# Decoder layer on one core: four last slabs by token tile, layer norm rows scaled on ScalarE, idle transposes on TensorE, and a first load of x of 256 columns

## What is computed

```python
h = layer_norm(ALPHA * x + 0.5 * swiglu(x, ffn1...), ln1_g, ln1_b)     # "up1", "down1"
mix = hybrid_mixer(h, ...)                                             # "kvdt", "attn", "attn_o", "ssd", "merge", "out"
h = layer_norm(ALPHA * h + mix, ln2_g, ln2_b)
h = layer_norm(ALPHA * h + 0.5 * swiglu(h, ffn2...), ln3_g, ln3_b)     # "up2", "down2"

def layer_norm(x, g, b):
    xc = x - mean(x)
    return xc * rsqrt(mean(xc * xc) + LN_EPS) * g + b
```

## Time and profile before

| | |
|---|---|
| time before, 3 runs | median 2670.36 us (2670.35 to 2671.6) |
| the profiled execution | 2668.99 us, span 2667.4 us |
| PE, PEld busy | 2634.5 us (99%), 2188.8 us (82%) |
| DVE busy | 2002.6 us (75%) |
| ACT busy | 1361.7 us (51%) |
| POOL busy | 130.0 us (5%) |
| chain that ended last | PE 95%, DVE 3%, ACT 1% |
| mean granted clock | 0.996 |

### The profile page before, as it was taken

One profiled execution on the slowest core, in us unless ns is written; L12 is line 12 of the kernel. 1 busy time (PEld: TensorE's weight loads), 2 busy tenths in 40 slices (PEclk: granted clock), 3 DMA queues, 4 the chain that ended last, 5 costly groups with the idle time before them and its releaser, 6 DMA issues.

```text
span 2667.4 us, 36687 instructions
## 1 busy us (share of the span) xinstructions
PE 2634.5 (99%) x12546; PEld 2188.8 (82%) x12546; DVE 2002.6 (75%) x2410; ACT 1361.7 (51%) x1678; POOL 130.0 (5%) x170
## 2 busy tenths in 40 slices
PE   8999999999999999999999999999999999999997
PEld 7888888888787788888888888888878888888886
DVE  6999997688666665677777765444689999977986
ACT  5555555455344454566555554444355555554553
POOL 1000000000000000211111100000000000000000
PEclk9999999999999999999999999999999999999999
DMA  6666566666655546665555565667666665666664
GB/s 224 204 191 209 185 205 204 214 200 204 189 171 147 156 150 197 206 181 179 177 177 177 179 183 165 190 190 247 200 190 204 190 211 186 205 202 229 210 208 171
DMA packets 286195, 513.96 MB, mean 193 GB/s; under 512 B 19648, under 2 KB 52592, under 8 KB 284048
## 3 DMA queue, kind: packets, MB, share of 16 engines
q1 hardware_dynamic: 279552, 485.03, 57.8%
q0 software_dynamic: 4880, 25.36, 2.6%
q10 hardware_dynamic: 1664, 2.26, 0.2%
HBM read 506.23 MB, written 6.36 MB: 192 GB/s over the span
## 4 chain that ended last, share of the span: by engine, by line
PE 95%; DVE 3%; ACT 1%; issue 0%; DMA 0%; POOL 0%; POOLq 0%; SPq 0%; ACTq 0%; DVEq 0%
PE acc L787 13%; PE acc L789 13%; PE acc L788 13%; PE acc L853 5%; PE acc L855 5%; PE acc L854 5%; PE acc L871 4%; PE acc L872 4%; PE acc L873 4%; PE spare L871 4%; PE spare L872 4%; PE spare L873 4%; PE spare L855 3%; PE spare L854 3%; PE spare L853 3%; PE spare L756 2%
## 5 line engine op out<-in xcount | busy, mean ns | idle before, releaser
L1728 DVE TENSOR_TENSOR w_lo<-land,w_hi 128x1024 fp32r<-128x1024 f32 (+1 forms) x956 | 1149.2, 1219 | 499.4 <-ACT w_hi L1309 490.6
L1309 ACT ACTIVATE w_hi<-land 128x1024 fp32r<-128x1024 f32 (+1 forms) x956 | 976.8, 1029 | 916.9 <-PE acc L789 328.0
L787 PE MATMUL acc<-w_hi,a_hi 128*128 128x512 f32 (+1 forms) x1184 | 451.2, 381 | 2.6 <-DVE a_lo L1775 1.8
L789 PE MATMUL acc<-w_hi,a_lo 128*128 128x512 f32 (+1 forms) x1184 | 435.8, 368 | 0.0
L788 PE MATMUL acc<-w_lo,a_hi 128*128 128x512 f32 (+1 forms) x1184 | 434.4, 367 | 0.0
L787 PEld LDWEIGHTS acc<-w_hi,a_hi 128*128 128x128 f32 x1184 | 223.9, 189 | 46.8 <-issue 9.2
L789 PEld LDWEIGHTS acc<-w_hi,a_lo 128*128 128x128 f32 x1184 | 223.6, 189 | 38.2
L788 PEld LDWEIGHTS acc<-w_lo,a_hi 128*128 128x128 f32 x1184 | 224.1, 189 | 37.4 <-issue 3.6
L853 PE MATMUL acc<-w_hi,a_hi 128*128 128x512 f32 x576 | 227.7, 395 | 2.0 <-DVE a_lo L1775 1.7
L855 PE MATMUL acc<-w_hi,a_lo 128*128 128x512 f32 x576 | 225.1, 391 | 0.0
L854 PE MATMUL acc<-w_lo,a_hi 128*128 128x512 f32 x576 | 225.0, 391 | 0.0
(11 more groups left out here) (388 smaller groups left out, 4233.1 us busy)
## 6 DMA issues: line engine op xcount, KB each, us to landing
land<-w_in SPq DMA_DIRECT2D x232, 512.0 KB, 3.9
land<-ffn_w_gate SPq DMA_DIRECT2D x176, 512.0 KB, 3.9
land<-ffn_w_up SPq DMA_DIRECT2D x176, 512.0 KB, 4.3
land<-ffn_w_down SPq DMA_DIRECT2D x176, 512.0 KB, 4.7
land<-w_ssd_o SPq DMA_DIRECT2D x64, 512.0 KB, 4.3
land<-w_in SPq DMA_DIRECT2D x132, 128.0 KB, 2.3
land<-w_attn_o SPq DMA_DIRECT2D x32, 512.0 KB, 4.1
land<-w_out SPq DMA_DIRECT2D x32, 512.0 KB, 4.4
```

Of the source, the lines that this page charges most:

```text
L787: pe.matmul(to, rows_hi, hi, start=first, stop=False)
L789: mm = pe.matmul(to, rows_lo, hi, start=False, stop=last)
L1309: act.activation(w_hi[:, l % SPLIT, 0:deep, 0:width], land[:, l % LAND, 0:deep, 0:width], ACT.Copy).then_inc(high, 1)
L1728: dve.tensor_tensor(w_lo[:, l % SPLIT, 0:deep, 0:width], land[:, l % LAND, 0:deep, 0:width], w_hi[:, l % SPLIT, 0:deep, 0:width].bitcast(F ...
```

## The change

Six edits:

1. `HALVED` goes from 3 to 4, in both seams and at the end of `down2`.
2. In `ln_first`, DVE normalises the two chunks of token tile 0 ahead of the split of the next slab 0, not behind it.
3. For the norms 1 and 2, ACT writes the scaled rows to `sz` (two halves), waits for itself, and copies them to `a_hi`; DVE's two halves of L1771 are gone and it only subtracts. `sz` has two places, so ACT waits for DVE's subtraction of tile u-2.
4. `keep_clock(n)` is new: n transposes of `ident` into a part of `acc` that nobody reads. Ten stand ahead of the first tile of x, 14 behind the eight blocks of token tile 0 and ten behind those of token tile 1 in each of the two seams.
5. The first load of x takes 256 columns (256 KB), the rest of the chunk follows behind slab 0.
6. In `up1` PE turns only tiles 0 and 1 ahead of slab 0, and tile l+2 (not l+4) behind slab l.

```diff
-HALVED = 3
+HALVED = 4
+WARM_START = 10
+WARM_GAP = (14, 10)
...
             def first_x(c):
-                sp.dma_start(resid[:, :, c * W:(c + 1) * W], x_view[:, :, c * W:(c + 1) * W]).then_inc(x_in[c], 16)
+                at = slice(2 * P if c == 0 else c * W, (c + 1) * W)
+                sp.dma_start(resid[:, :, at], x_view[:, :, at]).then_inc(x_in[c], 16)
-            first_x(0)
-            up(1, "up1", 0, {1: 1, 3: 2, 5: 3})
+            sp.dma_start(resid[:, :, 0:2 * P], x_view[:, :, 0:2 * P]).then_inc(x_first, 16)
+            up(1, "up1", 0, {1: 0, 2: 1, 3: 2, 5: 3})
...
+            def keep_clock(n):
+                for _ in range(n):
+                    pe.transpose(acc[:, 0, 0:P], ident[:, :], ident[:, :])
...
                 for t in range(TOK):
                     for u in range(4):
                         ln_turn_half(phase, u, x_no, t)
+                    keep_clock(WARM_GAP[t])
...
-                    pe.wait_ge(x_in[u // 2], 16)
+                    pe.wait_ge(x_first if u == 0 else x_in[u // 2], 16)
...
-                    if l + 4 < 8:
-                        ln_turn(ln, l + 4, x_no)
+                    ahead = 2 if x_no is None else 4
+                    if l + ahead < 8:
+                        ln_turn(ln, l + ahead, x_no)
...
-                    for u in range(4):
+                    for u in range(2):
                         ln_turn(ln, u, x_no)
...
+            keep_clock(WARM_START)
             ffn(1, "xT", None)
...
+                if u >= 2:
+                    read_bank(phase, 0, f"t{u - 2}")
+                h = sz[:, u % 2, :].rearrange("p (k n) -> p k n", k=2)
                 for k in range(2):
-                    last = act.activation(a_hi[:, 2 * u + k, :], two_tiles(bank)[:, k, :], ACT.Identity,
+                    last = act.activation(h[:, k, :], two_tiles(bank)[:, k, :], ACT.Identity,
...
-                last.then_inc(tile_hi, 1)
+                ch.link(last)
+                act.activation(a_hi[:, 2 * u:2 * u + 2, :], h, ACT.Copy).then_inc(tile_hi, 1)
...
-                for k in range(2):
-                    last = dve.tensor_scalar(h[:, k, :], two_tiles(bank)[:, k, :],
-                                             ln_col[:, cols, 2 * u + k:2 * u + k + 1],
-                                             ln_col[:, cols + 1, 2 * u + k:2 * u + k + 1], ALU.mult, ALU.add)
-                ch.link(last)
...
                     evacuate_half(phase, i, cc, scale, t, no)
+                    dve.wait_ge(ln_p, (no - 1) * TOK + t + 1)
+                    ln_part(t, 0)
+                    ln_part(t, 1)
                     if t == 0:
                         for l in range(EARLY_V):
                             split(after, 0, l)
-                    dve.wait_ge(ln_p, (no - 1) * TOK + t + 1)
-                    ln_part(t, 0)
-                    ln_part(t, 1)
```

More of the change, by code:

```diff
@@ L435, in build_decoder_layer @@
         x_in = [sem(f"x_in{c}") for c in range(NC_D)]
+        x_first = sem("x_first")
         par_in = sem("par_in")
@@ L1906, in mixed_rows @@
                 read_done(ln, 0, f"t{u}")
+                if s == 0:
+                    read_done(ln, 0, "t6")
+                    read_done(ln, 0, "t7")
                 at = slice(2 * u, 2 * u + 2)
```

## The result

The changed kernel takes 2675.78 us (median of 20 runs, 2674.13 to 2679.12) against 2670.36 us before (20 runs, 2668.80 to 2677.73): a ratio of 1.0020, 95% interval 1.0014 to 1.0026. It is **slower by 5.4 us**. My forecast was 2668.1, in a range up to 2672.2, with 0.03 for slower. It was wrong in sign and missed by 7.7 us.

A forecast was written before the change was run, and what follows sets the result against it. PE was taken as the bound, busy 99% of the span. Seams -1.73 and -1.66 and start +1.15 sum to -2.24: 2666.75 us for the profiled execution, 2668.1 for the median, range 2665.0 to 2672.2.

The forecast's parts named there:

- Scaled rows on ACT: Layer norm seams: moving the scaling from DVE to ACT starts slab 1 earlier, -1.73 us in the first, -1.66 in the second.
- two times 1.03 go, 3.04 are left: Layer norm 1 seam: of DVE's 5.10 us up to slab 1's split, two pairs of scaled halves vanish, leaving 3.04.
- for a loss that I don't see: Anywhere in the kernel: chance of 0.02 left for a loss not foreseen, no size given.
- The halved slabs and the earlier normalising: Seams and end of `down2`: tile 0's rows are normalised earlier, but PE's end does not move; worth 0.
- A + 6.2: Seams: PE can start slab 1 6.2 us after A, the time at which ACT starts on tile 0.
- Scaled rows at the seam: Seams: with ACT scaling, PE starts slab 0 2.53 us after ACT starts on tile 0, 0.37 earlier than before.
- idle transposes: Seams: both bursts are hidden and hold PE's full clock; if they don't hold it, the seam loses 0.2 us.
- Rival A: Seams: transposes do not hold the clock; +1.35 us in total, slower, 2671.7; chance 0.27.
- Rival D: Seams: ACT becomes the bound if its wait and copy take 1.3 us a tile; +1.35 in total, 2671.7; chance 0.05.
- The start, +1.15: Start: earlier first matmul -1.08, half clock +0.45, two more turned tiles +0.88, later `columns` +0.9; bounds -0.9 and +2.1.
- my 0.9: Start: `columns` must wait for DVE's subtraction of tile 7, now turned right ahead of the parameter rows; +0.9 us.
- I take 2.9: Start, slab 0: 2.9 us of matmuls at half clock instead of about 2, costing +0.45 us (bounds -1.0 and +0.95).

The follow-up runs named there:

- e1_code15: Changed kernel plus 15 tiny DVE memsets ahead of DVE's `ssd` loop, which then starts at 974 as before the change: 2666.51 us.
- e4_no_idle: e1_code15 without the idle transposes of the two seams (those at the start stay): 2669.28 us.
- e5_start_old: e1_code15 with the start as before the change (whole chunks of x, four tiles turned ahead of slab 0, no idle transposes there): 2664.93 us.
- e10_start_cold: e6_tile7_early without the ten idle transposes ahead of the first tile of x: 2665.45 us.
- e6_tile7_early: e1_code15 with tiles 2 and 3 turned behind slab 0, then tile l+3 behind slab l, so tile 7 comes a slab earlier: 2665.10 us.
- e12_code3: Changed kernel plus 3 DVE memsets in the place of e1_code15's 15, so DVE's `ssd` loop starts at 962: 2677.63 us in one run.
- e9_start_filled: e6_tile7_early with two more bursts of idle transposes in PE's wait for x, ten behind tile 0 and four behind tile 1: 2663.20 us.

## Why the prediction was wrong, and where it was right

**The step that failed** is in "Scaled rows on ACT": "two times 1.03 go, 3.04 are left". I priced the instructions that go from DVE by their duration and asked only what they free. That they also shorten the code in front of four of its five loops, I didn't ask, and no term of the sum, no rival and no doubt stood for it; the 0.02 "for a loss that I don't see" was all. It cost 2 x 5 = 9.9 us by the landmarks: 4.8 us of DVE at each jump (3.35 + 1.47), of which 3.10 reach PE as a rest, and 1.8 more behind it, most of it since PE's clock falls behind that rest. e1_code15 gives 9.3 of it back with 15 memsets of 0.23 us. The rest of the case is small beside it.

**The halved slabs and the earlier normalising, "Worth 0"**: too low. I looked at PE's wait of 0.24 us for tile 0's rows and at the chain from 718.13, but not at what DVE does between PE's end and 718.13: it had tile 0's rows in its queue ahead of tile 1's evacuation. The evacuation now starts 0.43 and not 0.86 behind the last matmul. So the seams gained 1.97 and 1.9 where I had 1.73 and 1.66; without those 0.4 my terms would have been a little high (slab 1 at A + 6.38, not A + 6.2).

**Scaled rows at the seam** and **idle transposes**: right, term by term (A + 2.54; clock 1.00 throughout; both bursts hidden). Rival A, that the transposes don't hold the clock, is refuted by e4_no_idle against e1_code15: 2.8 us by the medians, 3.1 by the landmarks, for two seams. Rival D is refuted by ACT's period of 1.59 us a tile (722.17 to 723.76) against my 1.65.

**The start, +1.15**: right in sign and nearly in size. e5_start_old puts it at 1.6 in the medians. The first matmul came at 8.61 (forecast 8.95), `columns` stood behind tile 7 as foreseen (0.87 for my 0.9), and PE was still held by a split at 53.26. The term that was mis-sized is the half clock in slab 0, "I take 2.9": it lasted 3.4 us from the first matmul in the profiled execution of the changed kernel (windows: 0.50 in 8.60 to 11.90, 1.00 from 12.00) and over 5 in that of e1_code15, whose start is the same (first matmul 8.82, the last of slab 0 at 13.65 still 0.43 behind the one before). In the first of these, tile 1 was turned at full clock at 7.15 (four transposes in 0.66 us), so ten idle transposes and tile 0 had brought the clock, and it fell again behind the rest of 2.18 us; in the second tile 1 took 1.11 us. That moves the start by over 1 us between executions, and goes with the +0.73 of one trace and the +2.00 of the other at the same landmark. My upper bound for the start was also added up wrong: its own terms, 0 + 0.95 + 0.88 + 0.9, give +2.7 and not +2.1.

Without the jumps' waits the kernel would have come to 2666.51 by e1_code15, inside my range and 1.6 below the forecast (3.0 below the kernel before beside it, where I had forecast 2.3). In part that is errors that cancel: by the landmarks the seams gave 0.4 more than I had, and the new start cost 0.4 to 0.8 more. The sum was sound for what it held; it held no term for code.

## What to carry to other kernels

Count the instructions of each engine ahead of every loop, before and after an edit, also where you only delete some: a loop that comes to lie over one more block of code can wait at every jump back (shown here for one loop of DVE, three blocks against four), and the sign in a profile is an idle time "<-issue" directly behind the branch together with more pieces on the queue of instructions. A few memsets in a hidden place move the loop off the edge, so try two or three places before you judge an edit by its time. And where PE rests for over 2 us and the clock falls, idle transposes are worth trying in all such gaps of a stretch at once, since one burst between long rests (e10_start_cold against e6_tile7_early) bought nothing.

## What the runs showed that I had not expected

- Code position is worth 9 to 11 us in a kernel of 2670, with no change in the work: 2666.51, 2665.68 and 2675.78 with 15, 7 and no memsets. With 3 it is 2677.63 in one run, 2 us worse than with none. Half of that is the start of its profiled execution (+1.1 at the landmarks against the changed kernel's), the other half the first jump (+1.0). It is not DVE's longer wait (4.25 + 2.59 instead of 4.21 + 1.37): PE's first matmul comes 11.1 us behind the branch in both kernels, and at the second jump, with waits as long, e12_code3 loses no more than the changed kernel. It is PE's clock, which is at 0.50 from 1321.7 to 1328.3, and in the changed kernel only from 1322.8 to 1326.1.
- DVE fetches its code in pieces of 128 instructions (8 KB), and a piece takes time: the first instruction behind a bad jump came 4.03 to 4.33 us after the branch in eight jumps of four kernels, against 0.28 in the kernel before.
- Idle transposes hold the full clock and also bring it: 1.29 us for ten in the second burst of e9_start_filled, 2.39 in the first. Matmuls behind them ran at 0.23 to 0.24 from the second on.
- Five pieces more per jump, where the loop lies in four blocks: the times fit one piece for each of the four and one for the block behind the loop, which would mean that three blocks and the next one stay at hand and four and the next one don't. The records don't name the blocks, so this is a reading and not shown.
- Left open: why executions differ by some 2 us in when the clock comes back in the start; this was not tried.
